# The second norm of a streaming encoder step computed inside the dense up stage

## The reference, cut to what matters

```python
def _rmsnorm(x, g):
    y = xf * lax.rsqrt(jnp.mean(xf * xf, axis=-1, keepdims=True) + EPS) * g
def _dense_ffn(x, g, w1, w3, w2):
    h = _rmsnorm(x, g)
    return x + (jax.nn.silu(h @ w1) * (h @ w3)) @ w2
```

## Time and profile before

| | us |
|---|---|
| median of 3 runs (5149.27 to 5151.6) | 5150.5 |
| the profiled execution, its own time | 5139.61 |
| its span, first to last instruction | 5138.3 |
| last matmul of mixout to first of the up stage | 58.34 |
| first to last matmul of the up stage | 530.65 |
| last matmul of the up stage to first of ffndown | 16.01 |

### The profile page before, as it was taken

How to read it: one execution, slowest core, us unless ns; L and a number is a source line. 1 busy time by engine, 2 the same in 40 slices (tenths; PEclk the granted TensorE clock), 3 DMA queues, 4 the chain that set the end, 5 groups by cost and what they waited for, 6 DMA issues and landing times. The chain is left out here.

```text
span 5138.3 us, 94405 instructions
## 1 busy us (share of the span) xinstructions
PE 4537.8 (88%) x38337; PEld 4273.2 (83%) x38337; DVE 1878.8 (37%) x2917; ACT 1621.6 (32%) x3026; POOL 976.7 (19%) x863
## 2 busy tenths in 40 slices
PE   5899997999887899979859788669999999999994
PEld 4789997888787899979836566669999999999993
DVE  3455404666522100011122322234445454455554
ACT  2573212333322000022200322334344444444442
POOL 0334323444332222313200001310000000000001
PEclk6899998999999899999979656889999999999997
DMA  1222225454242222134120000275556666676675
GB/s 43 63 67 89 93 89 123 99 118 99 59 139 63 75 71 63 59 107 121 56 58 14 1 0 26 75 198 158 158 160 176 173 186 176 171 202 179 177 208 197
DMA packets 975328, 563.49 MB, mean 110 GB/s; under 512 B 139201, under 2 KB 941346, under 8 KB 975090
## 3 DMA queue, kind: packets, MB, share of 16 engines
q1 hardware_dynamic: 909570, 486.33, 34.2%
q10 hardware_dynamic: 55344, 46.60, 3.2%
q0 software_dynamic: 10176, 27.19, 1.9%
HBM read 481.79 MB, written 77.93 MB: 109 GB/s over the span
## 5 line engine op out<-in xcount | busy, mean ns | idle before, releaser
L2220 DVE TENSOR_TENSOR experts_w_lo<-experts_raw,experts_w_hi 128x1024 fp32r<-128x1024 f32 x352 | 415.9, 1222 | 157.5 <-ACT experts_w_hi L2152 157.5
L209 PE MATMUL experts_pa<-experts_hx,experts_w_hi 128*128 128x272 f32 (+5 forms) x1408 | 410.4, 291 | 8.3 <-DVE experts_w_lo L2220 8.3
L209 PE MATMUL experts_pd<-experts_hid,experts_w_hi 128*128 128x272 f32 (+5 forms) x1408 | 411.2, 292 | 0.0
L209 PE MATMUL experts_pb<-experts_hx,experts_w_hi 128*128 128x272 f32 (+5 forms) x1408 | 408.2, 290 | 3.1 <-DVE experts_w_lo L2220 3.1
L210 PE MATMUL experts_pa<-experts_hx,experts_w_hi 128*128 128x272 f32 (+5 forms) x1408 | 408.7, 290 | 0.0
L211 PE MATMUL experts_pa<-experts_hx,experts_w_lo 128*128 128x272 f32 (+5 forms) x1408 | 408.7, 290 | 0.0
L211 PE MATMUL experts_pd<-experts_hid,experts_w_lo 128*128 128x272 f32 (+5 forms) x1408 | 407.9, 290 | 0.0
L210 PE MATMUL experts_pd<-experts_hid,experts_w_hi 128*128 128x272 f32 (+5 forms) x1408 | 407.7, 290 | 0.0
L210 PE MATMUL experts_pb<-experts_hx,experts_w_hi 128*128 128x272 f32 (+5 forms) x1408 | 407.5, 289 | 0.0
L211 PE MATMUL experts_pb<-experts_hx,experts_w_lo 128*128 128x272 f32 (+5 forms) x1408 | 407.5, 289 | 0.0
L209 PE MATMUL proj_pm<-hT,proj_w_hi 128*128 128x384 f32 (+1 forms) x1152 | 386.4, 335 | 14.6 <-POOL proj_w_lo L527 14.6
(11 more groups left out here) (398 smaller groups left out, 11196.2 us busy)
## 6 DMA issues: line engine op xcount, KB each, us to landing
experts_raw<-in_moe_w SPq DMA_DIRECT2D x352, 512.0 KB, 4.7
experts_raw<-in_moe_w SPq DMA_DIRECT2D x128, 704.0 KB, 5.9
projected<-proj_out SPq DMA_DIRECT2D x48, 544.0 KB, 3.7
proj_w<-in_gdn_w_in ACTq DMA_DIRECT2D x48, 512.0 KB, 4.1
ffnup_w<-in_ffn_w SPq DMA_DIRECT2D x44, 512.0 KB, 5.0
ffndown_w<-in_ffn_w SPq DMA_DIRECT2D x32, 704.0 KB, 4.7
mixout_w<-in_gdn_w_out SPq DMA_DIRECT2D x32, 512.0 KB, 4.0
delta_kkq<-projected SPq DMA_DIRECT2D x102, 128.0 KB, 2.9
```

Source lines behind the costliest of these rows:

```text
L209: pe.matmul(out, as_r(w_hi), as_r(x_hi), start=first, stop=False)
L2220: dve.tensor_tensor(as_r(w_lo[:, x, 0:KD, :]), raw[:, x, 0:KD, :], w_hi[:, x, 0:KD, :], ALU.subtract).then_inc(split[x], 1)
```

## The change

`tails_stage` and the call of norm1 are gone, and `ffn_up_stage` does both. ACT rounds x g at the start (x times the gain, with no root), DVE takes the rest of it, and PE's products run on these. Meanwhile ACT squares the feature tiles, DVE adds them up into one tile `total`, and PE sums it over partitions with three float32 matmuls (`x_sum`) that stand ahead of the k = 6 and k = 7 steps of the first b product. ACT takes Ln and Exp for the root `xr`. With it DVE multiplies every product by the root as it leaves PSUM (`scaled`): the a product into `arg`, which ACT then runs through silu in SBUF, and the b product into `hid`, which DVE multiplies by `arg` in a third step. PE's next a product waits for `a_taken` in place of `silued`.

The tails are turned by PE at the start of the stage and stored by SP behind the first weights. The weights come as one array `w_up`, laid out on the host by output tile, so that a tile is one DMA of 1 MB with 8 KB in a row for each partition; POOL prepares its w1 half and w3 half one after the other (128 x 1024 each), and reuses each half as soon as its own product is done. The first two tiles are written out; the loops start at turn 1.

Where code is left out below, a line holds only dots; the stages that are removed stand in full above.

```diff
...
-def tails_stage(nc, m, io):
...
-def ffn_up_stage(nc, m, hT, w1, w3):
...
+def ffn_up_stage(nc, m, io):
+    xT = m["xT"]
     with Stage(nc, "ffnup") as st:
+        hT = st.sb("hT", [P, 2, KD, TOK])
...
+        arg, hid = st.sb("arg", [P, TOK]), st.sb("hid", [P, 2, TOK])
+        total, xr = st.sb("total", [P, TOK]), st.sb("x_rinv", [P, TOK])
...
+        px = st.ps("px", [P, 2, 512])
+        kept_rows = hid[0:HIST * 32, 1, 0:2 * P].rearrange("p (a c) -> p a c", a=2)
...
+        w_loaded, w_rounded, w_split, stored = (two(n) for n in ("w_loaded", "w_rounded", "w_split", "stored"))
+        a_done, b_done, a_taken, silued, gated, passed, hid_step = (st.sem(n) for n in (
+            "a_done", "b_done", "a_taken", "silued", "gated", "passed", "hid_step"))
+        x_rounded, x_split, x_squared, x_added, x_summed, x_logged, x_rooted = (st.sem(f"x_{n}") for n in (
+            "rounded", "split", "squared", "added", "summed", "logged", "rooted"))
+        t_turned, t_copied, t_stored = (st.sem(f"tails_{n}") for n in ("turned", "copied", "stored"))
+        turned_tails = pm[0:HIST * 32, 1, 1, 0:2 * P].rearrange("p (a c) -> p a c", a=2)
+        squares = lambda k: total[:, :] if k == 0 else hid[:, 0, :] if k % 2 else arg[:, :]
+        gain = lambda k: m["gains"][:, G_FFN0 + k:G_FFN0 + k + 1]
...
             def _(sp):
...
+                def weights(i, u):
+                    sp.wait_ge(w_split[u], PRE + 2 * i)
+                    sp.dma_start(w[:, u, :, :, :], io["w_up"][bass.ds(2 * i + u, 1)].rearrange("o p x k c -> p (o x) k c")).then_inc(w_loaded[u], 16)
+                weights(0, 0)
+                weights(0, 1)
+                sp.wait_ge(t_copied, PRE + 1)
+                for a, name in enumerate(("conv_p", "conv_s")):
+                    sp.dma_start(io[name][0, 0].rearrange("j (t p) -> (j t) p", p=P), kept_rows[:, a, :]).then_inc(t_stored, 16)
+                with sp.Fori(1, KF // 2) as i:
...
+                        weights(i, u)
+                sp.wait_ge(t_stored, PRE + 32)
...
             def _(pool):
...
+                def prepare(i, u, again):
+                    pool.wait_ge(w_loaded[u], PRE + 16 * (i + 1))
+                    for x, freed in enumerate((a_done, b_done)):
+                        if again:
+                            pool.wait_ge(freed, PRE + 2 * i + u - 1)
+                            hold(pool, passed)
+                        split_weights(pool, w[:, u, x, :, :], w_hi[:, u, x, :, :], w_lo[:, u, x, :, :], w_rounded[u], w_split[u], 2 * i + x)
+                for u in range(2):
+                    prepare(0, u, False)
+                with pool.Fori(1, KF // 2) as i:
...
+                        prepare(i, u, True)
...
             def _(pe):
...
+                def piece(u, x, k):
+                    for b, (c, n) in enumerate(BLK):
+                        last = split_product(pe, pm[:, x, b, 0:n], w_hi[:, u, x, k, :], w_lo[:, u, x, k, :], hT[:, 0, k, c:c + n], hT[:, 1, k, c:c + n], k == 0, k == KD - 1)
+                    return last
+                def product(i, u, x):
+                    pe.wait_ge(w_split[u], PRE + 2 * i + x + 1)
+                    pe.wait_ge((a_taken, gated)[x], PRE + 2 * i + u)
+                    for k in range(KD):
+                        last = piece(u, x, k)
+                    last.then_inc((a_done, b_done)[x], 1)
+                def x_sum(b):
+                    s, n = BLK[b]
+                    pe.matmul(px[:, b % 2, 0:n], m["const"][:, C_ONES * P:(C_ONES + 1) * P], total[:, s:s + n], start=True, stop=True).then_inc(x_summed, 1)
+                for a in range(2):
+                    last = pe.transpose(turned_tails[:, a, :], m["tail"][:, a, :, :].rearrange("p j t -> p (j t)"), m["const"][:, 0:P])
+                last.then_inc(t_turned, 1)
+                pe.wait_ge(w_split[0], PRE + 1)
+                for k in range(KD):
+                    pe.wait_ge(x_split, PRE + k + 1)
+                    last = piece(0, 0, k)
+                last.then_inc(a_done, 1)
+                pe.wait_ge(w_split[0], PRE + 2)
+                pe.wait_ge(t_copied, PRE + 1)
+                for k in range(KD):
+                    if k == 6:
+                        pe.wait_ge(x_added, PRE + KD - 1)
+                        x_sum(0)
+                        x_sum(1)
+                    if k == 7:
+                        pe.wait_ge(x_logged, PRE + 1)
+                        x_sum(2)
+                    last = piece(0, 1, k)
+                last.then_inc(b_done, 1)
+                for x in range(2):
+                    product(0, 1, x)
+                with pe.Fori(1, KF // 2) as i:
...
+                        for x in range(2):
+                            product(i, u, x)
...
             def _(act):
+                def turn(i, u):
+                    act.wait_ge(a_taken, PRE + 2 * i + u + 1)
+                    act.activation(arg[:, :], arg[:, :], ACT.Silu).then_inc(silued, 1)
+                    act.wait_ge(gated, PRE + 2 * i + u + 1)
+                    act.dma_start(m["hid_dram"][bass.ds(2 * i + u, 1)].rearrange("o p t -> p (o t)"), hid[:, u, :]).then_inc(stored[u], 16)
+                for k in range(KD):
+                    act.activation(as_r(hT[:, 0, k, :]), xT[:, k, :], ACT.Copy, scale=gain(k)).then_inc(x_rounded, 1)
+                for k in range(KD):
+                    if k >= 3:
+                        act.wait_ge(x_added, PRE + k - 2)
+                    act.activation(squares(k), xT[:, k, :], ACT.Square).then_inc(x_squared, 1)
+                for b, (s, n) in enumerate(BLK):
+                    act.wait_ge(x_summed, PRE + b + 1)
+                    act.activation(xr[:, s:s + n], px[:, b % 2, 0:n], ACT.Ln, bias=m["eps"][:, :], scale=1.0 / D).then_inc(x_logged, 1)
+                act.wait_ge(x_logged, PRE + len(BLK))
+                act.activation(xr[:, :], xr[:, :], ACT.Exp, scale=-0.5).then_inc(x_rooted, 1)
...
+                        turn(i, u)
...
             def _(dve):
...
+                def scaled(to, x):
+                    (two, rest), (rtwo, rrest) = blocks3(to), blocks3(xr)
+                    dve.tensor_tensor(two, pm[:, x, 0:2, 0:384], rtwo, ALU.mult)
+                    return dve.tensor_tensor(rest, pm[:, x, 2, 0:320], rrest, ALU.mult)
+                def turn(i, u):
+                    dve.wait_ge(a_done, PRE + 2 * i + u + 1)
+                    dve.wait_ge(gated, PRE + 2 * i + u)
+                    scaled(arg, 0).then_inc(a_taken, 1)
+                    dve.wait_ge(b_done, PRE + 2 * i + u + 1)
+                    dve.wait_ge(stored[u], PRE + 16 * i)
+                    scaled(hid[:, u, :], 1).then_inc(hid_step, 1)
+                    dve.wait_ge(hid_step, PRE + 2 * i + u + 1)
+                    dve.wait_ge(silued, PRE + 2 * i + u + 1)
+                    dve.tensor_tensor(hid[:, u, :], hid[:, u, :], arg[:, :], ALU.mult).then_inc(gated, 1)
+                for k in range(KD):
+                    dve.wait_ge(x_rounded, PRE + k + 1)
+                    dve.scalar_tensor_tensor(out=as_r(hT[:, 1, k, :]), in0=xT[:, k, :], scalar=gain(k), in1=hT[:, 0, k, :],
+                                             op0=ALU.mult, op1=ALU.subtract).then_inc(x_split, 1)
+                dve.wait_ge(t_turned, PRE + 1)
+                dve.tensor_copy(kept_rows, turned_tails).then_inc(t_copied, 1)
+                for k in range(1, KD):
+                    dve.wait_ge(x_squared, PRE + k + 1)
+                    if k >= 2:
+                        dve.wait_ge(x_added, PRE + k - 1)
+                    dve.tensor_tensor(total[:, :], total[:, :], squares(k), ALU.add).then_inc(x_added, 1)
+                dve.wait_ge(x_rooted, PRE + 1)
+                turn(0, 0)
+                dve.wait_ge(t_stored, PRE + 32)
+                turn(0, 1)
+                with dve.Fori(1, KF // 2) as i:
...
+                        turn(i, u)
...
-    with sbt("h_ffn", [P, 2, KD, TOK], F32) as hT:
-        norm_stage(nc, m, "norm1", hT, G_FFN0, halves=True)
-        ffn_up_stage(nc, m, hT, io["ffn_w1"][0], io["ffn_w3"][0])
+    ffn_up_stage(nc, m, io)
...
+          "ffn_w2", "moe_router", "moe_w1", "moe_w3", "moe_w2", "final_norm"]
+TURNED = ["ffn_w1", "ffn_w3"]
...
             add_product_stage(nc, m, "mixout", m["og_dram"], HV, lambda to, t, p: [(to, w_out[p * V_DIM // 2:(p + 1) * V_DIM // 2, bass.ds(t * P, P)].rearrange("(k p) c -> p k c", p=P))])
-            tails_stage(nc, m, io)
...
+def laid_out(inputs):
+    up = [inputs[n][0].reshape(KD, P, KF, P).transpose(2, 1, 0, 3) for n in ("ffn_w1", "ffn_w3")]
+    return {"w_up": np.stack(up, axis=2)}
...
+    inputs = {n: np.asarray(inputs[n]) for n in INPUTS + TURNED}
...
+    arrays.update({f"in_{n}": np.ascontiguousarray(a) for n, a in laid_out(inputs).items()})
```

More of the change, by code:

```diff
@@ L1219, in _ @@
             def _(sp):
-                with sp.Fori(0, KF // 2) as i:
+                def weights(i, u):
[6 more added lines that the diff above has]
```

(34 more changed lines are left out.)

14 lines of the change are left out of this document (removed).

## The result

The kernel after takes **5103.85 us** (median; 5099.0 to 5107.5), the kernel before, beside it, 5149.9 (5143.6 to 5151.6): a ratio of 0.9912 with a 95% interval of 0.9895 to 0.9929. The direction was right. The forecast, 5110.7 with a range from 5106, lies above: 46 us were saved where I forecast 39.8. Yet the trace doesn't show 46. The profiled execution of after took 5103.35, that of before 5139.6, a difference of 36.3. The study is about this gap, and about the terms within it.

The account below looks back on a forecast made before the run. The prediction took a serial chain ahead of PE's first up product as the bound. PE ending 41.2 us earlier, less 1.35, saved 39.8: 5139.6 became 5099.8, plus a 10.9 offset gave 5110.7 us, range 5106 to 5119.

Parts of the forecast that it names:

- Entry and first weights: Ahead of the first up product: 1.3 us from mixout's last add to SP's issue, 5.1 until POOL has weights.
- POOL's first half: Before PE's first product: POOL's cast and subtraction of one 128 x 1024 half, 3.42 us alone, 5.54 beside DVE.
- POOL and DVE beside each other: At the up stage's entry: sharing SBUF with DVE's rests adds 1.06 us to each of two POOL instructions.
- The float32 sums: PE's three added float32 sums over 1088 columns in the up stage cost 2.2 us.
- The wait for the sum: PE before the first float32 sum, waiting for DVE's seventh add: 0.3 us charged, bounds 0 and 3.
- Rival C: Adds 3 us late, PE stands twice and the clock falls once: saved 34.4 us, 5116.1; chance 0.09.
- The wait for the root: PE stands 1.7 us before the second tile's a product, behind the last sum's chain; no clock loss taken.
- The end: Behind the up stage's last product, DVE's extra multiplication and a wait on itself cost 1.35 us.
- A: No sharing: POOL's first cast and subtraction run at their own pace; saved 42.3 us, 5108.2; chance 0.14.
- B: First weights land 5.5 us later, two 1 MB transfers sharing evenly; saved 34.3 us, 5116.2; chance 0.09.
- D: DVE's chain in the loop passes 12.06 us, so PE waits each tile; slower, 5161 at 14.5; chance 0.04.
- E: Products start only when the root is there, PE near 1676; saved 16 us, 5134; chance 0.02.

Follow-up runs that it names:

- early root: After, with POOL's second tile held until DVE's seventh add, sums two k steps earlier, root multiplied into silu's result in SBUF: 5101.7 us, ratio 0.9917.

## Why the prediction missed, step by step

- **What bounds the kernel:** right. The chain ahead of the first product was the whole gain, 57.45 - 11.14 = 46.3; the loop gave and lost nothing; the up stage's products gave 7.7 back (the sums, two waits and the lost clock) and its end 1.2, which leaves 37.4.
- **Entry and first weights:** 1.3 forecast, 1.70 measured (SP's issue); 5.1 forecast, 4.89 measured. Right within the bounds.
- **POOL's first half:** forecast 5.54, measured 4.50 (1644.58 to 1649.08). The cast, the first to come, paid nearly nothing, the subtraction 0.9. The first product came at 11.14 behind mixout instead of 12.08.
- **POOL and DVE beside each other:** the row's 1.06 for each POOL instruction was near: the later casts pay 1.06 (2.10 for 1.04), the subtractions 0.9, less than a full DVE instruction of 1.29 to 1.34; in the loop it is DVE's multiplication that pays, 3.26 on average for 1.29. By the rule of the Trainium skill (page "SBUF — State Buffer", section "Who interferes with whom") the later of two such instructions waits for the whole of the other; this trace shows waits somewhat short of that, and 0.1 for the first cast.
- **The float32 sums:** 2.2 forecast; 1.45 + 0.70 = 2.15 where the clock held.
- **The wait for the sum** was mis-sized: 0.3 forecast, 2.15 to 2.88 measured, inside my bounds of 0 to 3, plus 1.6 where the clock fell. DVE's chain from its first rest to its last add I had put at 1671.9 - 1638.2 = 33.7, and it took 33.9. That was luck: I had four of POOL's pairs, each shutting DVE out wholly (13.4 in all), and there were five at some 2.8 each (13.8). What failed is when the two sides of the race start. I had DVE 1.95 behind mixout's work, from an entry of 0.8, though I gave SP 1.3 for the same entry; ACT's first rounding came 1.73 behind it and DVE's first rest 2.96. And PE's first product came 0.9 earlier than forecast. Rival C had the late adds and the lost clock; it put the clock at 2.7.
- **The clock behind a wait.** I took rows 10 as showing a wait of 2.03 us without a loss, but read only the first matmul behind it. A little later in the same trace of before, the clock had fallen:

```profile
1431.56:1432.86 1.30, 1.30 (x10) 1.30 (x11) 1.30 (x3) 0.28 (x1) 0.00 (x0) 1.00 0.27 50
1433.00:1436.00 3.00, 3.00 (x15) 3.00 (x15) 1.38 (x3) 1.32 (x2) 0.00 (x0) 0.50 0.90 263
```

  So a row of before already spoke for rival C's lost clock. Behind the wait for the root, for which I used the row, no clock was lost all the same.
- **The wait for the root:** 1.7 forecast, 1.77 measured, and no clock lost behind it.
- **The loop:** nothing, as forecast, though DVE's multiplication takes 3.26 there.
- **The end:** 1.35 forecast; 1.17 between the first traces of before and after, 1.3 over all five, and 1.37 when the early root takes it back.
- **The sum:** 39.8 forecast for the stretch, 37.4 in the first trace of after, 38.0 over three.
- **The rivals:** A fell with POOL's 3.28, B with the 4.89, D with the loop without a gap, E with the first product at 11.14.
- **The step that failed** is the last line of it: "the median of the runs is 10.9 above it, and I carry the difference over". After's profiled execution stood 0.5 below its median, and 2.2 and 16.2 in its two other traces. From 5139.6 I forecast 39.8 and found 36.3, which is 3.5 the other way; the offset took 10.4 too much. Together that is the 6.9 by which the forecast was too high. I treated the distance of one execution from three as a property of the kernel, and the range of 5106 to 5119 took none of that doubt in. From the profile's own time the same sum would have given 5099.8; both ends belonged into the range.

Of the 46.0 us between the medians, 38.0 lie in the stretch. Some 2.7 more may be routing's. The rest stays open: before's level moves by 6 us between occasions, after's by 3, and no run separates that from a small saving outside the stretch.

## What to carry over

When a profiled execution and the shown runs of the same kernel disagree, that distance may be scatter until a second profile says otherwise: forecast the saving, and let the range reach from one base to the other. Work that is moved beside an engine that shares SBUF must be costed on both engines, with all that becomes free to start early; here one wait that held POOL back gave 3.8 us of the stretch. And the gain that was left lay in the same chain: loading the next stage's first weights under the stage before was worth 6.6 us of the stretch. A clock is read over the microseconds behind a wait, not from the first matmul.

## What I had not expected of the hardware

- The granted clock fell behind a wait of 2.15 us on PE (0.68 over the next 5 us; 0.66 in the second trace) and not behind waits of 2.55 and 2.88 in the same place (1.00). In before's mixout it fell 1.3 us after the end of a wait of 2.03. The length of the wait alone doesn't decide it.
- Which engine pays for the sharing differs: in the entry both do (POOL 2.10 for 1.04 and 3.3 for 2.40, DVE 2.12 to 3.45 for a rest of 1.34); in the loop POOL's subtraction keeps its 2.40 and DVE's multiplication takes 3.26 instead of 1.29.
- Routing, which was not edited, took 84.0 to 86.9 us in the eight traces with the new up stage and 87.3 to 88.4 in the three with the old one.
